# DeepNorm decoder layer on one core: places of their own for the last six value tiles, the last columns in quarters, arrays placed at multiples of 128 bytes

## What is computed

```python
# per token: 16 of 16384 experts for each of 8 heads, gates by softmax
hid = gelu(einsum('cd,chkd->chk', xc, u_tab[ec]))
h   = einsum('chk,chkd->cd', gate * hid, v_tab[ec])
x   = layer_norm(ALPHA * x + h, ln2_g, ln2_b)
```

## Time and profile before

| | |
|---|---|
| runs | 1075.8, 1078.66, 1080.53 us |
| profiled execution | 1075.98 us, span 1074.2 us |
| TensorE matmul busy | 1060.0 us (99%) |
| VectorE, ScalarE, GpSimd busy | 787.0 (73%), 610.1 (57%), 172.2 (16%) us |
| DMA | 186.48 MB, mean 174 GB/s |
| mean granted TensorE clock | 0.998 |

### The profile page before, as it was taken

One profiled execution on the slowest core, in us unless ns is written; L12 is line 12 of the kernel. 1 busy time (PEld: TensorE's weight loads), 2 busy tenths in 40 slices (PEclk: granted clock), 3 DMA queues, 4 the chain that ended last, 5 costly groups with the idle time before them and its releaser, 6 DMA issues.

```text
span 1074.2 us, 17959 instructions
## 1 busy us (share of the span) xinstructions
PE 1060.0 (99%) x5580; PEld 903.8 (84%) x5580; DVE 787.0 (73%) x1511; ACT 610.1 (57%) x1116; POOL 172.2 (16%) x119
## 2 busy tenths in 40 slices
PE   8999999999999999999999999999999999999996
PEld 6888888878888888888889999988888888888885
DVE  4458767577999998999999988875555555555556
ACT  4347646565456666666766666655544455555543
POOL 3040002012000022233233355500000000000001
PEclk9999999999999999999999999999999999999999
DMA  8555444444455554544444444455666555555553
GB/s 283 185 191 165 141 149 153 157 143 158 156 177 190 193 179 160 168 163 157 156 162 152 141 151 138 137 176 190 200 199 211 197 195 195 194 190 194 190 191 116
DMA packets 52857, 186.48 MB, mean 174 GB/s; under 512 B 6336, under 2 KB 6976, under 8 KB 52816
## 3 DMA queue, kind: packets, MB, share of 16 engines
q1 hardware_dynamic: 51152, 181.82, 50.9%
q0 software_dynamic: 944, 3.15, 0.9%
q10 hardware_dynamic: 720, 1.05, 0.3%
HBM read 184.94 MB, written 1.05 MB: 173 GB/s over the span
## 4 chain that ended last, share of the span: by engine, by line
PE 91%; DVE 3%; DMA 2%; ACT 1%; POOL 1%; issue 1%; POOLq 0%; ACTq 0%; SPq 0%; DVEq 0%
PE ps L1490 22%; PE ps L1492 11%; PE ps L1586 10%; PE ps L1587 10%; PE ps L1588 10%; PE ps L1258 6%; PE ps L1260 5%; PE ps L1259 5%; PE ps L1541 5%; DVE wlo L791 1%; PE ps L1319 1%; DMA raw<-w_tiles_v 1%; DMA xraw<-xT 1%; ACT whi L485 1%; PE ps L1506 0%
## 5 line engine op out<-in xcount | busy, mean ns | idle before, releaser
L791 DVE TENSOR_TENSOR wlo<-raw,whi 128x1024 fp32r<-128x1024 f32 x341 | 425.0, 1247 | 238.3 <-ACT whi L485 235.7
L485 ACT ACTIVATE whi<-raw 128x1024 fp32r<-128x1024 f32 x343 | 363.5, 1060 | 283.1 <-DMA raw<-w_tiles_v 166.7
L1490 PE MATMUL ps<-pair,whi 128*128 128x512 f32 x1152 | 411.9, 400 | 0.1
L1492 PE MATMUL ps<-pair,wlo 128*128 128x256 f32 x1152 | 321.7, 279 | 0.0
L1490 PEld LDWEIGHTS ps<-pair,whi 128*128 128x128 f32 x1152 | 216.2, 188 | 46.5 <-issue 0.3
L1492 PEld LDWEIGHTS ps<-pair,wlo 128*128 128x128 f32 x1152 | 217.5, 189 | 0.0
L1586 PE MATMUL ps<-whi,hhi 128*128 128x512 f32 x512 | 199.4, 389 | 0.8 <-DVE wlo L791 0.7
L1588 PE MATMUL ps<-whi,hlo 128*128 128x512 f32 x512 | 199.2, 389 | 0.0
L1587 PE MATMUL ps<-wlo,hhi 128*128 128x512 f32 x512 | 199.2, 389 | 0.0
L462 POOL TENSOR_TENSOR hot_j<-raw_ij,gateT 128x512 f32<-128x512 bf16 x64 | 120.8, 1888 | 331.0 <-DVE raw_ij L1163 331.0
L674 ACT ACTIVATE low<-ps 128x256 f32<-128x256 f32 x144 | 55.0, 382 | 139.6 <-PE ps L1492 138.2
(11 more groups left out here) (212 smaller groups left out, 876.7 us busy)
## 6 DMA issues: line engine op xcount, KB each, us to landing
raw<-w_tiles_u SPq DMA_DIRECT2D x128, 512.0 KB, 3.3
raw<-w_tiles_v SPq DMA_DIRECT2D x128, 512.0 KB, 3.3
raw<-w_tiles_in SPq DMA_DIRECT2D x63, 512.0 KB, 3.3
raw<-w_tiles_q SPq DMA_DIRECT2D x16, 512.0 KB, 3.3
raw<-w_tiles_out SPq DMA_DIRECT2D x8, 512.0 KB, 3.2
xt<-x POOLq DMA_DIRECT2D x1, 1024.0 KB, 6.8
raw<-w_tiles_in SPq DMA_DIRECT2D x2, 256.0 KB, 4.1
xraw<-xT SPq DMA_DIRECT2D x2, 256.0 KB, 7.4
```

The source lines that it names most:

```text
L485: act.activation(whi[:, tile.slot, :], raw[:, tile.slot, :], ACT.Copy)\
L791: dve.tensor_tensor(wlo[:, tile.slot, :], raw[:, tile.slot, :], whi[:, tile.slot, :].bitcast(F32), ALU.subtract)\
L1490: pe.matmul(ps[:, bank, :], whi[:, tile.slot, cols], pair[:, k, :, :].rearrange("p a n -> p (a n)"), start=k == 0, stop=False)
L1492: last = pe.matmul(ps[:, bank, SEQ:2 * SEQ], wlo[:, tile.slot, cols], ahi[:, k, :], start=False, stop=k == KC - 1)
```

## The change

- The last LATE = 6 value tiles (122 to 127) leave the ring. Their raw data, remainders, high parts and their rows of H in two parts get places over rows 0 to 59 of H. SyncE loads one of them after the loads of value tiles 71, 79, 87, 95, 103 and 111, without a wait of its own. ScalarE and VectorE split one of them after each of the ring tiles 111, 113, 115, 117, 119 and 121, which are written out from 111 on.
- TensorE takes ring tiles up to 121 whole, then the six late tiles part by part: t = 0 first half (18 matmuls of 512 columns), t = 0 second half (18), t = 1 first half (18), t = 1 third quarter of the columns (18 matmuls of 256 columns), t = 1 last quarter (18 of 256), the last into bank 0, which VectorE has read by then.
- VectorE adds and takes statistics in the same parts; of the last quarter the ring tiles' sum is added ahead, and the late tiles' sum when it is there.
- `stats` grows from 96 to 192 bytes, and `work_at` is rounded to 128 instead of 64.
- `norm` is split into functions; the first layer norm calls them in the same order as before.

```diff
-    stats = place("stats", [P, NT, 2, 6])
+    stats = place("stats", [P, NT, 4, 6])
...
-    at[0] = (at[0] + 63) // 64 * 64
+    at[0] = (at[0] + 127) // 128 * 128
     work_at = at[0]
...
+    late_raw = place("late_raw", [P, LATE, W], alias=work_at)
+    late_lo = place("late_lo", [P, LATE, W], F32R, alias=work_at)
+    late_hi = place("late_hi", [P, LATE, W], F32R, alias=work_at + 4 * LATE * row)
+    late_hhi = place("late_hhi", [P, LATE, SEQ], F32R, alias=work_at + 8 * LATE * row)
+    late_hlo = place("late_hlo", [P, LATE, SEQ], F32R, alias=work_at + 9 * LATE * row)
... SyncE
+        for n in range(LATE):
+            at = LATE_FROM + n * LATE_EVERY
+            rounds(T_V, w_tiles_v, at, at + LATE_EVERY)
+            sp.dma_start(late_raw[:, n, :], w_tiles_v[RINGED + n, :, :]).then_inc(late_full[n], 16)
... ScalarE
+        for m in range(LATE_SPLIT, RINGED):
+            split_h(Tile(T_V + m))
+            split_hi(Tile(T_V + m))
+            n, odd = divmod(m - LATE_SPLIT, 2)
+            if not odd:
+                act.activation(late_hhi[:, n, :], H[:, RINGED + n, :], ACT.Copy).then_inc(S["late_hi_ready"], 1)
+                act.wait_ge(late_full[n], 16)
+                act.activation(late_hi[:, n, :], late_raw[:, n, :], ACT.Copy).then_inc(S["late_hi_ready"], 1)
... VectorE, after split_h and split_lo of tile m
+                dve.wait_ge(S["late_hi_ready"], 2 * n + 1)
+                dve.tensor_tensor(late_hlo[:, n, :], H[:, RINGED + n, :], late_hhi[:, n, :].bitcast(F32),
+                                  ALU.subtract).then_inc(S["late_lo_ready"], 1)
+                dve.wait_ge(S["late_hi_ready"], 2 * n + 2)
+                dve.tensor_tensor(late_lo[:, n, :], late_raw[:, n, :], late_hi[:, n, :].bitcast(F32), ALU.subtract)\
+                    .then_inc(S["late_lo_ready"], 1)
+        for half in range(2):
+            dve.wait_ge(S["value_done"], half + 1)
+            total(0, half * CW, CW, ps[:, VB[half], :])
+        variance(1, 0, 2)
+        scale_first(1)
+        dve.wait_ge(S["value_done"], 3)
+        total(1, 0, CW, ps[:, VB[2], :], 2)
+        dve.wait_ge(S["value_done"], 4)
+        total(1, CW, QW, ps[:, VB[3], 0:QW])
+        own.do(dve.scalar_tensor_tensor(out=xt[:, 1, CW + QW:D], in0=xt[:, 1, CW + QW:D], scalar=ALPHA,
+                                        in1=ps[:, VB[3], QW:CW], op0=ALU.mult, op1=ALU.add))
+        dve.wait_ge(S["value_done"], 5)
+        own.do(dve.tensor_tensor(xt[:, 1, CW + QW:D], xt[:, 1, CW + QW:D], ps[:, VB[0], 0:QW], ALU.add))
+        own.step(dve.bn_stats(stats[:, 1, 3, :], xt[:, 1, CW + QW:D]))
+        variance(1, 1, 4)
+        apply_second(1, LN2_BANKS, "g2_ready", "out_ready")
... TensorE (before: t = 0 of the last 3 tiles, then t = 1 by halves)
+        for half in range(2):
+            for n in range(LATE):
+                if half == 0:
+                    pe.wait_ge(S["late_lo_ready"], 2 * n + 2)
+                last = late_values(n, 0, half * CW, CW, ps[:, VB[half], :], False, n == LATE - 1)
+            last.then_inc(S["value_done"], 1)
+        for first, width, bank in ((0, CW, ps[:, VB[2], :]), (CW, QW, ps[:, VB[3], 0:QW])):
+            for n in range(LATE):
+                last = late_values(n, 1, first, width, bank, False, n == LATE - 1)
+            last.then_inc(S["value_done"], 1)
+        pe.wait_ge(S["ln_var"], NT + 1)
+        for n in range(LATE):
+            last = late_values(n, 1, CW + QW, QW, ps[:, VB[0], 0:QW], n == 0, n == LATE - 1)
+        last.then_inc(S["value_done"], 1)
```

More of the change, by code:

```diff
@@ L87 @@
 TAIL = 3
+LATE = 6
+LATE_FROM, LATE_EVERY = 64, 8
+RINGED = TILES_V - LATE
+LATE_SPLIT = 111
 Y_TURN, Y_LATE = T_OUT - 1, 1
@@ L316, in layer @@
     OUTB = (6, 7, 0, 1)
-    names = ("raw_full0 raw_full1 raw_full2 raw_full3 raw_first zeros_ready hi_first lo_first in_xT0 in_xT1 in_xT2 in_xT3 in_xT4 in_lr in_x in_small "
+    names = ("raw_full0 raw_full1 raw_full2 raw_full3 raw_first late_full0 late_full1 late_full2 late_full3 late_full4 late_full5 late_hi_ready late_lo_ready value_done zeros_ready hi_first lo_first in_xT0 in_xT1 in_xT2 in_xT3 in_xT4 in_lr in_x in_small "
              "in_ln1 in_ln2 hi_ready lo_ready lo_first_q tiles_used evac_act evac_dve consts "
@@ L329, in layer @@
     raw_full = [S[f"raw_full{n}"] for n in range(NS)]
+    late_full = [S[f"late_full{n}"] for n in range(LATE)]
     in_xT = [S[f"in_xT{n}"] for n in range(X_PARTS)]
@@ L358, in _, with rounds @@
             sp.dma_start(dst, src).then_inc(S["in_small"], 16)
[L359 to L362, removed]
+        def rounds(first, src, begin, end):
+            with sp.Fori(begin // NS, end // NS) as i:
                 for k in range(NS):
                     load(Tile(first + k, i, NS), src[bass.ds(i * NS + k, 1), :, :].rearrange("a p n -> p (a n)"))
+        for first, n, src, skip in ((0, TILES_IN, w_tiles_in, NS), (T_OUT, TILES_OUT, w_tiles_out, 0),
+                                    (T_Q, TILES_Q, w_tiles_q, 0), (T_U, TILES_U, w_tiles_u, 0),
+                                    (T_V, LATE_FROM, w_tiles_v, 0)):
+            rounds(first, src, skip, n)
+        for n in range(LATE):
+            at = LATE_FROM + n * LATE_EVERY
+            rounds(T_V, w_tiles_v, at, at + LATE_EVERY)
+            sp.dma_start(late_raw[:, n, :], w_tiles_v[RINGED + n, :, :]).then_inc(late_full[n], 16)
+        rounds(T_V, w_tiles_v, LATE_FROM + LATE * LATE_EVERY, RINGED // NS * NS)
+        for m in range(RINGED // NS * NS, RINGED):
+            load(Tile(T_V + m), w_tiles_v[m, :, :])
         for half in range(2):
@@ L770, in _ @@
                 value_tiles(LN2_COPIES + 2 * n + half, LN2_COPIES + 2 * n + half + 1)
[L771 to L774, removed]
+        value_tiles(LN2_COPIES + 4, (LATE_SPLIT - AHEAD) // 4)
+        for m in range(LATE_SPLIT, RINGED):
[6 more added lines that the diff above has]
+                act.activation(late_hi[:, n, :], late_raw[:, n, :], ACT.Copy).then_inc(S["late_hi_ready"], 1)
         own.do(act.activation(gate_warm[:, :], ident[:, 0:1], ACT.Sqrt))
@@ L993, in _, with total, variance, scale_first @@
                 y_low(3)
[L994 to L1014, removed]
+        def total(t, first, width, bank, parts=1):
+            xs = xt[:, t, first:first + width]
+            own.do(dve.scalar_tensor_tensor(out=xs, in0=xs, scalar=ALPHA, in1=bank, op0=ALU.mult, op1=ALU.add))
+            size = width // parts
+            for part in range(first, first + width, size):
+                own.step(dve.bn_stats(stats[:, t, part // size, :], xt[:, t, part:part + size]))
+        def variance(n, t, groups):
+            own.wait()
+            own.do(dve.bn_aggr(mv[:, t, :], stats[:, t, 0:groups, :].rearrange("p a b -> p (a b)")))
+            dve.tensor_scalar(rstd[:, t:t + 1], mv[:, t, 1:2], LN_EPS, None, ALU.add)\
+                .then_inc(S["ln_var"], 1)
+        def scale_first(n):
             dve.wait_ge(S["ln_sqrt"], NT * n + 1)
@@ L1018, in norm, with apply_second @@
                                      op0=ALU.mult, op1=ALU.mult).then_inc(S["ln_shift"], 1)
[L1019 to L1023, removed]
+        def apply_second(n, gain, gain_ready, done):
             dve.wait_ge(S[gain_ready], 4)
@@ L1047, in _ @@
         dve.wait_ge(S["in_x"], 16)
-        norm(0, OUTB, LN1_BANKS, "x1_bank", "g1_ready", T_Q, "ln_done")
+        dve.wait_ge(S["x1_bank"], 1)
+        total(0, 0, CW, ps[:, OUTB[0], :])
+        dve.wait_ge(S["half_done"], 1)
+        total(0, CW, CW, ps[:, OUTB[1], :])
+        variance(0, 0, 2)
+        scale_first(0)
+        dve.wait_ge(S["x1_bank"], 2)
+        total(1, 0, CW, ps[:, OUTB[2], :])
+        dve.wait_ge(S["tiles_used"], T_Q)
+        total(1, CW, CW, ps[:, OUTB[3], :])
+        variance(0, 1, 2)
+        apply_second(0, LN1_BANKS, "g1_ready", "ln_done")
         x1_low()
@@ L1238, in _ @@
             split_lo(Tile(T_V + k + AHEAD))
-        with dve.Fori(1, TILES_V // 4 - 1) as i:
+        with dve.Fori(1, (LATE_SPLIT - AHEAD) // 4) as i:
             for k in range(4):
@@ L1243, in _ @@
                 split_lo(tile)
[L1244 to L1247, removed]
+        for m in range(LATE_SPLIT, RINGED):
+            split_h(Tile(T_V + m))
+            split_lo(Tile(T_V + m))
+            n, odd = divmod(m - LATE_SPLIT, 2)
+            if not odd:
+                dve.wait_ge(S["late_hi_ready"], 2 * n + 1)
[20 more added lines that the diff above has]
+        apply_second(1, LN2_BANKS, "g2_ready", "out_ready")
     @block.tensor
@@ L1577, in _, with value_part, values, late_values @@
         hidden(after(CHUNKS - 1) + 1, TILES_U)
-        def values(tile, t, start, stop, halves=(0, 1)):
+        def value_part(o, hh, hl, wh, wl, start, stop):
+            pe.matmul(o, hh, wh, start=start, stop=False)
+            pe.matmul(o, hh, wl, start=False, stop=False)
+            return pe.matmul(o, hl, wh, start=False, stop=stop)
+        def values(tile, t, start):
             tok = slice(t * P, (t + 1) * P)
```

(26 more changed lines are left out.)

## The result

Eleven runs of each: 1082.69 us median (1081.6 to 1085.06) against 1077.24 (1075.8 to 1080.53), ratio 1.0055, interval 1.0046 to 1.0064. The forecast was 1076.0, a little faster; the change costs about 5.9 us by the ratio (5.0 to 6.9 by its interval) and 5.5 by the medians.

What follows compares the result with a forecast made beforehand. TensorE's string of matmuls bounds nearly all of the kernel, with two chains side by side at its end. SyncE's store 1.58 us earlier plus 0.68 gave 2.26 us off; from median and mean, 1076.0 us, range 1072.5 to 1079.5.

Steps and rivals of the forecast that it cites:

- Alignment: Arrays after the small ones begin 128 bytes later, still at a multiple of 128; claimed worth nothing either way.
- the sum: At the kernel's end: SyncE's store 1.58 us earlier plus the 0.68 it was ahead, 2.26 us off.
- last sign: In the value tiles, a TensorE pace other than 0.2264 us would mean placement matters and the forecast is wrong.
- Rival B: Value tiles: late loads take the ring's time and it starves, 5.4 us slower, 1084; chance 3%.
- B's sign: Idle on TensorE between value tiles 72 and 121 would show that late loads starve the ring.
- Late loads: Value tiles: six loads come earlier, each delaying a ring load 0.1 to 0.3 us of 2.2 spare; cost nothing.
- Late splits: ScalarE and VectorE among the ring tiles: extra splits cut the spare 2.2 us to 1.5; TensorE should not stand.
- the 0.99 us: TensorE's stall and slow restart at the last three tiles, claimed to go since late tiles are ready.
- Quarters: End of t = 1: 36 matmuls of 256 columns at 0.12 us replace 18 of 512, costing 0.24 us.
- rival A: Quarters at the end: 256-column matmuls held up by their loads, 2.5 to 5.8 us more, 1078.5 to 1081.8; 7%.
- Tail of t = 1: After TensorE's last matmul: VectorE's combination of statistics and the chain to the stores come earlier, taken as 1.58 us.
- Tail of t = 0: GpSimd's chain at the end: starts at 1056.7, ends by 1066.8, so hidden; SyncE's store ends the program.

Runs made afterwards that it cites:

- e2: Changed kernel with H and all that follows back at the old address 76,160, the larger stats at the top of memory: 1075.01 us, ratio 0.9978.
- e4: Changed kernel with only the ring of H's high and low parts 128 bytes further: 1075.37 us, ratio 0.9979 to the kernel before.
- e8: Changed kernel with start and work_at rounded up to multiples of 256 bytes: 1075.05 us, ratio 0.9977 to the kernel before.
- s1: Kernel before with the four slots of H's high and low parts offset by 0, 64, 128 and 192 bytes: 1081.83 us, one run.
- s2: Kernel before with the four slots of H's high and low parts offset by 256, 320, 384 and 448 bytes: 1081.47 us, one run.
- e3: Kernel before with only the ring of H's high and low parts 128 bytes further: 1085.12 us, ratio 1.0069.
- e1: Kernel before with proj, H and all that follows 128 bytes further, nothing else: 1085.5 us, ratio 1.0074.

## Why the prediction was wrong

**The step that failed is "Alignment".** It said that the arrays began at a multiple of 128 already, that they now begin 128 bytes later, and that this is "worth nothing, either way", since a faster VectorE would win nothing under a busy TensorE. The first two are right. The step that fails is the price of nothing: its only reason was about VectorE, and the move took the stationary operand from distance 0 to distance 128 of the moving one. I asked what an address does to VectorE and ScalarE, and not what it does to TensorE, the one engine that bounds the kernel. What the traces show in its place is 0.2333 us a matmul instead of 0.2267 in all ring tiles.

The two traces account for the size. From the start of the first value matmul to that of the last one of tile 121 the changed kernel takes 341.47 us and the kernel before 332.05: 9.42 more. From there to the end it takes 23.74 against 25.87: 2.13 less. The stages ahead are 0.45 us shorter. Together that is 6.8, the difference of the two spans; the medians differ by 5.5, and the interval of the ratio reaches from 5.0 to 6.9 us.

**The pace was taken as a constant.** All of the sum rested on 0.2264 us a matmul. The prediction named this as its last sign ("A TensorE pace other than 0.2264 in the value tiles would mean that the placement matters after all, and the forecast would be wrong"), and gave it no chance among the rivals. Rival B names 1084 us, near what was measured, but that is coincidence: B's sign was idle on TensorE between value tiles 72 and 121, and there is none.

**The other steps held.** Late loads: no idle of TensorE in the value tiles, so rival B falls. Late splits: no stall between tile 121 and the end; the 0.99 us went. Quarters: 0.120 us each, as taken, so rival A falls. With it falls the rule of the Trainium skill that was weighed there ("TensorE: Matmul & The Clock Gate", section "The mechanism"): 36 matmuls over all 128 rows, each with a load of its own, start 0.120 us apart, where 256 columns at 2.4 GHz are 0.107. The prediction left out that the same section of the Trainium skill also lets a load into the background weight buffer run ahead, which would fit this pace; no run shows which buffer was used. Tail of t = 1: 7.05 us from the last matmul to the end, against 6.98 reckoned (1071.94 less 1064.96). Tail of t = 0: hidden, since GpSimd ends at 1074.7 and SyncE's stores begin at 1077.9. With the placement put right, e2, e4 and e8 measure 0.9977 to 0.9979, that is 2.3 to 2.5 us, and the ends of their traces, behind tile 121, are 2.1 to 2.2 us shorter than before; the sum said 2.26.

## What to carry to other kernels

Where TensorE bounds a kernel, treat the addresses of its stationary and moving operands as part of its speed: measure the distance from one start to the next before and after any edit that moves an array, be it 96 bytes of statistics. Put the two operands at the same place modulo 256 bytes, and don't trust "an aligned address"; this is shown here for fp32r matmuls of 512 columns, 128 rows and a load for each. And when a table shows an engine 100% busy with a different count of the same instruction, compare counts per microsecond: busy time alone hides the loss.

## What the runs showed of the hardware that I had not expected

Back-to-back fp32r matmuls of 512 columns, each with its own load of the stationary operand, start 0.2267 us apart when both operands have the same address modulo 256 bytes (places 0, 128 and 192 were seen), and 0.229 to 0.234 at distances of 32 to 224; 256 bytes more change nothing (s1 and s2). Why is not shown. The end of e3 rules out writes into the two rings as the cause; a conflict of TensorE's own two reads is the obvious guess, and only guessed. The Trainium skill ("TensorE: Matmul & The Clock Gate", "Wait — 56ns, not 53.3ns?") gives 215.7 ns for 512 columns back to back at the full clock; no matmul of 512 columns here was followed sooner than after 224 ns.

Two things stay open. One is the pace at a given distance: the changed kernel and e1 have their operands at the same bytes and differ by 0.0009 us a matmul. The other is that the pairs of the hidden layer have more than one pace without any change of address: between 325 and 375 us they take 346.7 ns in the kernel before and 353.3 in e2, whose `pair` and `whi` lie at the same bytes. The traces' means over the stage, 348 to 351 ns, would make an estimated 4 us over its 1152 pairs. That is of the size of the scatter between runs of one kernel (1072.3 to 1079.2 in e4), but with one trace of each kernel it is not shown that the scatter comes from there. What puts TensorE into the one or the other pace was not tried.
